# Two-layer hybrid backbone step: weighing with V as the stationary operand in two column groups, a bank for each head's transposes, and loads and splits at the layer boundary in another order

## The chip, the cores and the metric

The kernel runs on one core of one Trainium2 chip. The metric is the device time of one execution, in microseconds; several executions are timed and the median is given. One further execution is recorded by the hardware profiler.

## What is computed

640 tokens (512 latent, 128 of context) go through two layers. A layer is three parallel token mixers behind one projection (an attention with windows and sinks, a gated MLP over chunks, an attention over all keys), gated and merged, and then an expert-choice channel mixer with 16 experts. The part that the change touches is the attention:

```python
def softmax_with_sink(s, sink):                 # sink is None in the second attention
    sk = sink[:, :, None, None]
    m = jnp.maximum(jnp.max(s, axis=-1, keepdims=True), sk)
    e = jnp.exp(s - m)
    return e / (jnp.sum(e, axis=-1, keepdims=True) + jnp.exp(sk - m))

sc = jnp.einsum('bqkgd,btkd->bkgqt', qi, k) * (HEAD_DIM ** -0.5)
p = softmax_with_sink(sc, sink)
o = jnp.einsum('bkgqt,btkd->bqkgd', p, v)       # "weighing"
merged = (gates[:, :, 0] * (oa @ w_a_o) + gates[:, :, 1] * (ob @ w_b_o)
          + gates[:, :, 2] * (oc @ w_c_o))
```

Each attention has 6 query heads of 64 and 2 key heads (kv), so a kv head serves 3 query heads. All data are 32-bit floats.

## The kernel before

**Tiles and pairs.** Tokens stand in NT = 5 tiles of 128 rows (four latent, one of context). A *pair* j is one tile t, one branch br (0: windowed, 1: all keys) and one g of 0 to 2, that is the two heads (kv 0, g) and (kv 1, g). There are NP = 30 pairs in a layer. Its keys come in blocks of 128: in branch 0 three or four for the latent tiles (the cache is one of them), in branch 1 five; one for the context tile. That is 108 blocks in a layer.

**The attention loop** runs over steps j = 0 to 30, and the order on every engine is written out by hand. In step j TensorE computes scores(j) (banks 0 to 3), then turn(2j-2) and turn(2j-1), the transposes of the two heads' exponentials of pair j-1 into PSUM from column 1536 on, for both heads the same place, and then weigh(j-1), which multiplies them with V into bank 5. Between these stand three gaps, which the list FILL fills with other work: gate groups (24 matmuls into bank 6), output projections ("proj", bank 7), the gated MLP and transposes ("side" work, all through bank 7, in a fixed order with one user at a time). VectorE does in step j: peak(j), the maximum over the scores; in gap 0 its part of the filling; turned(j-1), the copy of head 0's transposes; weights(j-1), the reciprocal of the sum; and weighed(j-1), which scales bank 5 by that reciprocal while copying it into the buffer AO. ScalarE does exps(j, 0), turned(j-1) for head 1 and exps(j, 1). When the three pairs of a tile are done, the item "out" transposes AO (three transposes through bank 7) and ScalarE copies it into qoT, where the projection reads it.

Semaphores tie this together: e_ready counts exponentials, pt_done transposes, pt_evac their copies, pv_done weighings, o_evac their copies.

**The tail.** What is left of gates and projections follows the loop in a list TAIL, then the output matrix, the router, the choice of tokens and the experts.

**The experts** stream 2 MB chunks of weights through a ring of three slots on SP's queue. Every chunk is split into a rounded part (ScalarE, hi) and a rest (VectorE, lo) before TensorE uses it. POOL's queue gathers the tokens for each expert and scatters the results into x in HBM (indirect DMAs).

**The layer boundary.** ScalarE waits for the last scatter, loads x back (five tiles), squares each (L1115), takes roots (L1119), then splits two units of the projection's weights (L1141). VectorE computes means, normalises two tiles (L1471), does its part of the first split (L1459) and only then modcol (L1482, L1484), for which the evacuation of the first transposes (L1182) waits. POOL issues nine parameter loads at the start of each layer. SP loads the first two projection chunks and a chunk of the modulation weights once the last weight split of the experts is done.

**Lines.** Scores L834, transposes of exponentials L854, weighing L870, gate groups L753, projections L891, side transposes L693, modulation matmuls in four column groups of 32 L707, peak L1581 to L1586, exponentials L1248, evacuations L1259 (ScalarE) and L1594 (VectorE), weighed L1613, outputs' copy L1283, experts L1050.

Of the kernel before, what the change touches and what calls it, by code (L numbers as in the profile page):

```python
# [5 lines left out]
D = 1024  # L6
KB = D // 128
NS = 4
NT = NS + 1
DEPTH = 2  # L10
HD = 64
# [7 lines left out]
E = 16  # L19
# [122 lines left out]
for n in range(2 * NT - 1):  # L142
    put(3 * n + 4, 0, "out", n)
# [7 lines left out]
TAIL.insert(0, ("out", 2 * NT - 1))  # L151
# [6 lines left out]
def build(nc, A, outs, scratch):  # L158
# [10 lines left out]
    with ctx:  # L169
# [95 lines left out]
        AO = SC[:, 768:1536].rearrange("p (b k n) -> p b k n", b=2, k=2)  # L265
# [26 lines left out]
        psf = ps.rearrange("p b n -> p (b n)")  # L292
        s_pair = psf[:, 0:1792].rearrange("p (k c) -> p k c", k=2)
# [7 lines left out]
        PARS = 9  # L301
# [63 lines left out]
        pt_evac = sem("pt_evac")  # L365
# [156 lines left out]
        def _(pool):  # L522
# [12 lines left out]
            for l in range(DEPTH):  # L535
# [3 lines left out]
                par(wsraw, A["b_ws"][l].rearrange("g p q -> p g q"))  # L539
                par(gain.rearrange("p a b d -> p (a b d)"), A["qk_gain"][bass.ds(l, 1)].to_broadcast([128, 4 * HD]))  # L540
                par(vgain[:, :], A["b_v_norm"][bass.ds(l, 1)].to_broadcast([128, 256]))
                par(sink[:, :], A["a_sink"][bass.ds(l, 1)].to_broadcast([128, 6]))
                par(brt[:, :], A["b_router"][bass.ds(l, 1)].to_broadcast([128, E]))
                par(bs[:, :], A["b_bs"][l])
                par(cacheV[:, :, :], A["cache_v"][l])
                par(ckraw, A["cache_k"][l])
                par(wr[:, :, :], A["w_router"][l].rearrange("(k p) n -> p k n", p=128))
# [126 lines left out]
                for e in range(3):  # L674
                    gather(e)
                for e in range(E):
# [6 lines left out]
        def _(pe):  # L683
# [12 lines left out]
            for l in range(DEPTH):  # L696
# [91 lines left out]
                for g in range(QG):  # L788
# [7 lines left out]
                    if g == NT:  # L796
                        pe.wait_ge(par_ready, l * 16 * PARS + 16 * PARS)
                        side("ws", 0)
# [48 lines left out]
                def turn(v):  # L847

                    n = len(pair(v // 2)[3])
                    pe.wait_ge(e_ready, l * UNITS + v + 1)  # L850
                    if l or v:
                        pe.wait_ge(pt_evac, l * UNITS + v)
                    for i in range(n):
                        last = nc.tensor.transpose(psf[:, 1536 + 128 * i:1536 + 128 * i + 128],  # L854
# [3 lines left out]
                def weigh(j):  # L858

                    t, br, g, blocks = pair(j)  # L860
                    pe.wait_ge(pt_evac, l * UNITS + 2 * j + 2)
# [19 lines left out]
                def project(o):  # L881
# [27 lines left out]
                def outputs(n):  # L909

                    pe.wait_ge(o_evac, l * NP + 3 * n + 3)
                    side("out", n)
                    a = AO[:, n % 2].rearrange("p k n -> p (k n)")
                    transposes(7, [a[:, 128 * i:128 * i + 128] for i in range(3)], side_done)

                def merged_tile(t):

                    pe.wait_ge(merged_ready, l * 8 * NT + 7 * NT + t + 1)
                    if t == 0:
                        pe.wait_ge(e_ready, (l + 1) * UNITS)  # L920
                        pe.wait_ge(pt_evac, (l + 1) * UNITS)
                    turn_tile(H_M, t, cols2(merged[:, t]))

                def extra(kind, i):
# [9 lines left out]
                    elif kind == "out":  # L934
                        outputs(i)
# [167 lines left out]
        def _(act):  # L1103
# [7 lines left out]
            for l in range(DEPTH):  # L1111
# [13 lines left out]
                for t in range(NT):  # L1125
                    act.wait_ge(x_in[t], l * 16 + 16)
                    square(0, t)
                for t in range(NT):
                    root(t, rs5[:, t:t + 1], st5[:, t:t + 1])
# [44 lines left out]
                split(1)  # L1174
                act.wait_ge(modcol_ready, l + 1)
# [77 lines left out]
                def turned(j):  # L1253
# [5 lines left out]
                    nc.scalar.activation(probT[:, 1, 0:n], psf[:, 1536:1536 + n], ACT.Copy).then_inc(pt_evac, 1)  # L1259
# [19 lines left out]
                def outputs_out(n):  # L1279

                    br, t = divmod(n, NT)
                    act.wait_ge(side_done, l * NSIDE + SIDE["out", n] + 1)
                    nc.scalar.activation(qoT[:, 3 * br:3 * br + 3, 128 * t:128 * t + 128],  # L1283
                                         ps[:, 7, 0:384].rearrange("p (s n) -> p s n", s=3), ACT.Copy).then_inc(side_free, 1)

# [6 lines left out]
                def extra(kind, i):  # L1292
# [3 lines left out]
                    elif kind == "out":  # L1296
                        outputs_out(i)
# [107 lines left out]
        def _(dve):  # L1405
# [14 lines left out]
            for l in range(DEPTH):  # L1420
# [52 lines left out]
                for t in range(NT):  # L1473
                    mean(0, t)
                normalise(0)
                normalise(1)
                split(0)
# [8 lines left out]
                dve.wait_ge(modcol_ready, l + 1)  # L1486

# [377 lines left out]
```

## Time and profile before

| what | value |
|---|---|
| median of 3 runs | 2658.25 us (2649.14 to 2659.18) |
| the profiled execution | 2648.39 us |
| its span | 2646.6 us |
| TensorE (PE) busy | 2370.5 us, 90% |
| VectorE (DVE) busy | 1577.5 us, 60% |
| ScalarE (ACT) busy | 1195.9 us, 45% |
| DMA | 566.08 MB, 214 GB/s over the span |

Layer 0's mixers run from the start to about 740 us, its experts to 1335 us, layer 1's mixers from 1344 to about 2060 us and its experts to the end. The attention loops lie from about 211 to 548 us and from 1519 to 1858 us. Where this text counts a matmul in f32 on the trace, it is two rows, and so are its weight loads. Durations of matmuls overlap; what one takes from the engine is seen in the distance between starts.

### The profile page before, as it was taken

The numbers are of one execution on the slowest core, as the hardware profiler recorded it, in microseconds if no ns is written. First come the engines' busy times: TensorE is split into PE (matmuls) and PEld (weight loads), VectorE is DVE, ScalarE is ACT, GpSimd is POOL, SyncE is SP. The second block draws the span as 40 slices with busy tenths as digits, with TensorE's granted clock in tenths as the row PEclk, the third lists the DMA queues.
The fourth block names the chain that finished last, engine by engine and source line by source line (L and its number), as shares of the span: only waits on it lengthen the run. The fifth ranks groups of instructions, "written<-read, shape, count | busy, mean of one in ns | idle before, by whom it ended". The sixth has DMA issues, their size and how long they took to land.

```text
span 2646.6 us, 36927 instructions
## 1 busy us (share of the span) xinstructions
PE 2370.5 (90%) x14645; PEld 1837.7 (69%) x14645; DVE 1577.5 (60%) x1807; ACT 1195.9 (45%) x1368; POOL 326.4 (12%) x246
## 2 busy tenths in 40 slices
PE   3998899999859999999849988999995999999997
PEld 1777779989636666666537777898995566666664
DVE  1244434334648888888832453343246788888885
ACT  3223223222246666676632332233122666676674
POOL 1012000000020112221111020000003012111211
PEclk8999999999979999999969999999996999999998
DMA  8351110023589999999844510101044899999995
GB/s 320 128 178 49 50 57 33 4 85 136 193 294 341 369 372 367 371 376 373 320 159 160 175 52 19 56 33 57 33 175 147 288 357 370 372 380 373 370 377 187
DMA packets 268317, 566.08 MB, mean 214 GB/s; under 512 B 7496, under 2 KB 9608, under 8 KB 268144
## 3 DMA queue, kind: packets, MB, share of 16 engines
q1 hardware_dynamic: 251776, 509.63, 53.3%
q0 software_dynamic: 14512, 48.05, 6.3%
q10 hardware_dynamic: 1904, 6.62, 0.7%
q8 instruction: 92, 1.51, 0.2%
q14 instruction: 33, 0.27, 0.0%
HBM read 542.71 MB, written 24.18 MB: 214 GB/s over the span
## 4 chain that ended last, share of the span: by engine, by line
PE 35%; DMA 19%; DVE 7%; ACT 5%; issue 5%; DVEq 0%; ACTq 0%; SPq 0%; POOL 0%; POOLq 0%
PE ps L1050 13%; PE ps L753 12%; DMA ring<-in_w_down 9%; DMA ring<-in_w_up 8%; DVE w_lo L1768 5%; ACT w_hi L1360 3%; PE ps L891 3%; PE ps L870 2%; PE ps L834 1%; PE ps L693 1%; DVE EP L1783 1%; PE ps L854 1%; DMA X<-x_save 0%; PE ps L707 0%; DMA ring<-in_w_gate 0%
## 5 line engine op out<-in xcount | busy, mean ns | idle before, releaser
L1768 DVE TENSOR_TENSOR w_lo<-ring,w_hi 128x2048 fp32r<-128x2048 f32 x378 | 859.2, 2285 | 161.2 <-ACT w_hi L1360 158.4
L1360 ACT ACTIVATE w_hi<-ring 128x2048 fp32r<-128x2048 f32 x384 | 720.5, 1911 | 356.4 <-DMA ring<-in_w_down 165.1
L1050 PE MATMUL ps<-w_hi,xT 128*80 128x512 f32 x2048 | 649.9, 396 | 5.5 <-issue 3.2
L753 PE MATMUL ps<-WH,HTH 128*128 128x256 f32 x1840 | 543.8, 296 | 14.5 <-ACT Y L1277 9.0
L753 PE MATMUL ps<-ringL,HTH 128*128 128x256 f32 x1840 | 523.2, 284 | 0.0
L753 PE MATMUL ps<-WH,HTL 128*128 128x256 f32 x1840 | 522.2, 284 | 0.0
L1050 PEld LDWEIGHTS ps<-w_hi,xT 128*80 128x80 f32 x2048 | 305.9, 149 | 179.0 <-issue 9.8
L1050 PE MATMUL ps<-w_lo,xT 128*80 128x512 f32 x1024 | 405.9, 396 | 0.0
L753 PEld LDWEIGHTS ps<-WH,HTH 128*128 128x128 f32 x1840 | 355.1, 193 | 41.4 <-issue 23.4
L753 PEld LDWEIGHTS ps<-ringL,HTH 128*128 128x128 f32 x1840 | 355.4, 193 | 0.9
L753 PEld LDWEIGHTS ps<-WH,HTL 128*128 128x128 f32 x1840 | 354.2, 192 | 0.0
L1050 PE MATMUL ps<-w_hi,hT 128*80 128x512 f32 x1024 | 329.0, 397 | 25.6 <-DVE hT L1774 12.3
L1050 PEld LDWEIGHTS ps<-w_hi,hT 128*80 128x80 f32 x1024 | 153.1, 149 | 116.3 <-issue 14.7
L1050 PEld LDWEIGHTS ps<-w_lo,xT 128*80 128x80 f32 x1024 | 153.1, 150 | 80.3 <-issue 2.5
L1050 PE MATMUL ps<-w_lo,hT 128*80 128x512 f32 x512 | 203.0, 396 | 0.0
L891 PE MATMUL ps<-ring,QK 128*128 128x256 f32 x640 | 163.2, 388 | 16.0 <-ACT QK L1283 6.4
L1459 DVE TENSOR_TENSOR ringL<-ring,WH 128x2048 fp32r<-128x2048 f32 x46 | 105.4, 2290 | 111.1 <-ACT WH L1141 110.8
L891 PEld LDWEIGHTS ps<-ring,QK 128*128 128x128 f32 x640 | 112.5, 190 | 37.0 <-DVE Y L1632 9.9
L1277 ACT ACTIVATE SC<-ps 128x256 f32<-128x256 f32 x80 | 30.6, 383 | 226.9 <-PE ps L753 226.8
L1634 DVE SCALAR_TENSOR_TENSOR SC<-SC,ps 128x256 f32<-128x256 f32 x80 | 33.7, 421 | 157.9 <-PE ps L891 157.9
L1141 ACT ACTIVATE WH<-ring 128x2048 fp32r<-128x2048 f32 x46 | 87.6, 1909 | 74.0 <-PE ps L753 69.3
L671 POOL DMA_INDIRECT out<-EP,idx x16 | 62.4, 3898 | 455.0 <-DVE EP L1783 455.0
(198 smaller groups left out, 2303.7 us busy)
## 6 DMA issues: line engine op xcount, KB each, us to landing
ring<-in_w_gate SPq DMA_DIRECT2D x64, 2048.0 KB, 9.5
ring<-in_w_up SPq DMA_DIRECT2D x64, 2048.0 KB, 9.5
ring<-in_w_down SPq DMA_DIRECT2D x64, 2048.0 KB, 11.5
ring<-in_w_mod SPq DMA_DIRECT2D x23, 2048.0 KB, 7.9
ring<-in_w_in SPq DMA_DIRECT2D x18, 2048.0 KB, 7.8
ring<-in_w_out SPq DMA_DIRECT2D x4, 2048.0 KB, 9.4
ring<-in_w_o SPq DMA_DIRECT2D x4, 1536.0 KB, 6.4
Y<-x_save POOLq DMA_DIRECT2D x10, 512.0 KB, 7.1
```

The source lines that it names most:

```text
L671: pool.indirect_dma_start(x_out[l], bass.IndirectOffsetOnAxis(ap=idx[0:CE, e:e + 1], axis=0), eo[0:CE, e % 2], None, compute_op=ALU.add).t ...
L693: last = nc.tensor.transpose(ps[:, bank, 128 * i:128 * i + 128], s, ident[:, :])
L753: last = nc.tensor.matmul(dst, a[:, t, k], w, start=k == 0 and i == 0, stop=k == KB - 1 and i == 2)
L870: last = nc.tensor.matmul(ps[:, 5, 64 * kv:64 * kv + 64], probT[:, kv, 128 * i:128 * i + 128], v, start=i == 0, stop=i == len(blocks) - 1)
L891: last = nc.tensor.matmul(ps[:, 7, 0:256], qoT[:, k, 128 * t:128 * t + 128], w[:, i, 256 * q:256 * q + 256], start=i == 0, stop=k == ks[-1])
L1050: last = nc.tensor.matmul(ps[0:CE, bank], lhs[:, a, kb], w[:, u, k], start=kb == 0 and i == 0, stop=kb == KB - 1 and i == 2)
L1141: nc.scalar.activation(WH[:, u % 2], unit_cols(l, u, ring), ACT.Copy).then_inc(wa_hi, 1)
L1277: nc.scalar.activation(dst, ps[:, 6, 0:256], ACT.Tanh, scale=0.5).then_inc(gs_ready, 1)
L1360: nc.scalar.activation(w_hi[:, u % UB], ring[:, raw[0], 4 * (u % 2):4 * (u % 2) + 4], ACT.Copy).then_inc(hi_ready, 1)
L1459: TT(unit_cols(l, u, ringL), unit_cols(l, u, ring), WH[:, u % 2].bitcast(f32), ALU.subtract).then_inc(wa_lo, 1)
L1634: STT(gated, gate_s[:, o % 2], 1.0, ps[:, 7, 0:256], ALU.add, ALU.mult).then_inc(side_free, 1)
L1768: TT(w_lo[:, u % UB], ring[:, raw[0], 4 * (u % 2):4 * (u % 2) + 4], w_hi[:, u % UB].bitcast(f32), ALU.subtract).then_inc(lo_ready, 1)
```

## The change

Weighing takes V (128 keys by 64) as the stationary operand and streams the transposed weights (128 columns). The two heads of a pair go to two column groups, rows 0 to 63 and 64 to 127 of bank 5, so that the output comes out already transposed, and is copied straight into qoT. The transposes "out", their copies and AO are gone; the rows of the output weights are put in the order of the pairs on the host. As the scale of a query now lies along columns, the exponentials are scaled before they are transposed: weights(j-1) comes to the start of VectorE's step and does two multiplications. In branch 0 the two heads' transposes get a bank each. At the boundary, seven of nine parameter loads for layer 1 are issued during layer 0's experts, ScalarE's and VectorE's first splits stand ahead of the norms, the first chunks' loads wait for different counts, and the modulation chunk waits for x.

```diff
-for n in range(2 * NT - 1):
-    put(3 * n + 4, 0, "out", n)
-TAIL.insert(0, ("out", 2 * NT - 1))
-        AO = SC[:, 768:1536].rearrange("p (b k n) -> p b k n", b=2, k=2)
+        turned_at = lambda v: 1536 + (512 * (v % 2) if pair(v // 2)[1] == 0 else 0)
-        PARS = 9
+        PARS = 7
...
                 for c, slot in PRE[l]:
-                    if BEFORE[l][c] is None:
-                        sp.wait_ge(lo_ready, l * UNITS_E + 1)
-                    else:
+                    if BEFORE[l][c] is not None:
                         released(BEFORE[l][c])
+                    elif l:
+                        sp.wait_ge(lo_ready, l * UNITS_E + 1 - 2 * (RING - 1 - slot))
+                    if c == ("mod", 0):
+                        sp.wait_ge(x_in[NT - 1], 16 * (l + 1))
...
+                def load_params(l):
+                    par(gain.rearrange("p a b d -> p (a b d)"), A["qk_gain"][bass.ds(l, 1)].to_broadcast([128, 4 * HD]))
+                    par(vgain[:, :], A["b_v_norm"][bass.ds(l, 1)].to_broadcast([128, 256]))
+                    par(sink[:, :], A["a_sink"][bass.ds(l, 1)].to_broadcast([128, 6]))
+                    par(brt[:, :], A["b_router"][bass.ds(l, 1)].to_broadcast([128, E]))
+                    par(bs[:, :], A["b_bs"][l])
+                    par(cacheV[:, :, :], A["cache_v"][l])
+                    par(wr[:, :, :], A["w_router"][l].rearrange("(k p) n -> p k n", p=128))
+                raw(wsraw, A["b_ws"][l].rearrange("g p q -> p g q"))
+                raw(ckraw, A["cache_k"][l])
+                if l == 0:
+                    load_params(0)
...
                 for e in range(3):
                     gather(e)
+                if l + 1 < DEPTH:
+                    load_params(l + 1)
...
                 def turn(v):
-                    pe.wait_ge(e_ready, l * UNITS + v + 1)
-                    if l or v:
-                        pe.wait_ge(pt_evac, l * UNITS + v)
+                    pe.wait_ge(p_ready, l * UNITS + v + 1)
+                    if v // 2 >= NP // 2 or v // 2 == 0:
+                        for b in range(2):
+                            if l * NP + (v + 1 - b) // 2:
+                                pe.wait_ge(pt_evac[b], l * NP + (v + 1 - b) // 2)
+                    else:
+                        pe.wait_ge(pt_evac[v % 2], l * NP + v // 2)
...
                 def weigh(j):
-                    for kv in range(2):
-                        for i, b in enumerate(blocks):
+                    for i, b in enumerate(blocks):
+                        for kv in range(2):
...
-                            last = nc.tensor.matmul(ps[:, 5, 64 * kv:64 * kv + 64], probT[:, kv, 128 * i:128 * i + 128], v,
-                                                    start=i == 0, stop=i == len(blocks) - 1)
+                            last = nc.tensor.matmul(ps[64 * kv:64 * kv + 64, 5, 0:128], v,
+                                                    probT[:, kv, 128 * i:128 * i + 128], start=i == 0,
+                                                    stop=i == len(blocks) - 1, tile_position=(0, 64 * kv))
...
                 def project(o):
+                    if s:
+                        pe.wait_ge(o_evac, l * NP + 3 * ((s - 1) * NT + t) + 3)
...
                 # ScalarE
+                if l == 0:
+                    norms()
...
                 split(0)
                 split(1)
+                if l:
+                    norms()
...
                 # VectorE
+                if l == 0:
+                    norms()
+                    split(0)
...
                 dve.wait_ge(modcol_ready, l + 1)
+                if l:
+                    split(0)
+                    norms()
...
                 def weights(j):
+                    for kv in range(2):
+                        TS(prob[:, kv, 0:n], prob[:, kv, 0:n], rden[:, b, kv:kv + 1], None, ALU.mult).then_inc(p_ready, 1)
                 def weighed(j):
-                    TT(AO[:, n % 2, :, 64 * g:64 * g + 64], ps[:, 5, 0:128].rearrange("p (k d) -> p k d", k=2),
-                       rden[:, j % 2, :, None].to_broadcast([128, 2, HD]), ALU.mult).then_inc(o_evac, 1)
+                    nc.vector.tensor_copy(qoT[:, 3 * br + g, 128 * t:128 * t + 128], ps[:, 5, 0:128]).then_inc(o_evac, 1)
                 for j in range(NP + 1):
+                    if j:
+                        weights(j - 1)
                     if j < NP:
                         peak(j)
...
-                    if j:
-                        weights(j - 1)
```

## Rows read from the trace of the kernel before

**Rows 1.** Windows of three stages: length, busy (records) of each engine, clock, DMA

```profile
210.00:330.00 120.00, 103.05 (x776) 92.86 (x775) 55.31 (x121) 38.36 (x90) 16.24 (x25) 0.91 0.14 46
400.00:535.00 135.00, 132.35 (x1117) 125.15 (x1116) 54.27 (x101) 41.57 (x88) 0.00 (x0) 1.00 0.09 32
780.00:1000.00 220.00, 213.50 (x980) 138.06 (x981) 186.53 (x122) 149.94 (x111) 26.75 (x11) 0.99 1.02 360
```

**Rows 2.** Grouped lines of TensorE by shape: busy us, mean ns, idle before

```profile
L891 PE MATMUL ps<-ring,QK 128*128 128x256 f32 x640 | 163.2, 388 | 16.0 <-ACT QK L1283 6.4 <-DVE Y L1632 5.4 <-DVE Y L1621 3.2
L870 PE MATMUL ps<-Y,EP 128*128 128x64 f32 x672 | 92.8, 276 | 5.3 <-ACT EP L1259 5.3
L834 PE MATMUL ps<-QK 64*128 64x128 f32 x864 | 76.5, 301 | 4.8 <-ACT EP L1248 3.2 <-issue 1.6
L854 PE MATMUL ps<-ident,EP 128*128 128x128 f32 x432 | 67.4, 274 | 9.0 <-DVE EP L1594 7.7 <-ACT EP L1248 1.3
L870 PE MATMUL ps<-cacheV,EP 128*128 128x64 f32 x192 | 38.1, 281 | 0.0
...
L693 PE MATMUL ps<-ident,SC 128*128 128x128 f32 x90 | 15.5, 281 | 5.7 <-DVE Y L1632 3.1 <-ACT QK L1203 1.7 <-DVE SC L1613 0.9
```

**Rows 3.** Timeline of TensorE in the second branch, layer 0: start, duration, instruction

```profile
469.21 0.71 PE L854 MATMUL ps<-ident,EP 128*128 128x128 f32 x5
...
469.76 1.46 PE L891 MATMUL ps<-ring,QK 128*128 128x256 f32 x6
...
471.05 1.00 PE L870 MATMUL ps<-Y,EP 128*128 128x64 f32 x8
...
473.32 1.39 PE L834 MATMUL ps<-QK 64*128 64x128 f32 x20
...
474.64 0.38 PE L753 MATMUL ps<-WH,HTH 128*128 128x256 f32 x1
...
477.57 0.60 PE L854 MATMUL ps<-ident,EP 128*128 128x128 f32 x4
```

**Rows 4.** Timeline of TensorE around a modulation matmul in column groups

```profile
1391.90 0.28 PE L753 MATMUL ps<-WH,HTL 128*128 128x256 f32 x1
1392.11 1.92 PE L707 MATMUL ps<-ring,condT 128*32 128x512 f32 x16
1393.96 0.39 PE L753 MATMUL ps<-WH,HTH 128*128 128x256 f32 x1
1394.18 0.28 PE L753 MATMUL ps<-ringL,HTH 128*128 128x256 f32 x1
```

**Rows 5.** What the exponentials (L1248) waited for: us, times

```profile
PE ps L854: 62.2, 32
DVE nm L1586: 11.7, 4
```

**Rows 6.** Timeline at the layer boundary

```profile
1344.33 2.40 ACTq L1124 DMA_DIRECT2D X<-x_save  x5
...
1359.46 1.06 ACT L1115 ACTIVATE QK<-X 128x1024 f32<-128x1024 f32 x1 [1.10 <-DMA X<-x_save]
1360.42 0.19 ACT L1115 ACTIVATION_READ_ACCUMULATOR QK<-X 128x1 f32 x1
...
1362.40 3.70 ACT L1141 ACTIVATE WH<-ring 128x2048 fp32r<-128x2048 f32 x2
...
1363.21 1.94 PE L693 MATMUL ps<-ident,QK 128*128 128x128 f32 x8 [27.84 <-issue]
...
1364.33 2.29 DVE L1459 TENSOR_TENSOR ringL<-ring,WH 128x2048 fp32r<-128x2048 f32 x1 [0.36 <-ACT WH L1141]
...
1367.16 1.50 ACT L1182 ACTIVATE EP<-ps,modcol 128x128 f32<-128x128 f32 x4 [1.07 <-DVE modcol L1484]
...
1368.63 0.75 DVE L1471 TENSOR_SCALAR QK<-X,rs 128x1024 f32<-128x1024 f32 x1
```

**Rows 7.** DMA issues, 1320 to 1365 us: KB each, median us to landing

```profile
X<-x_save ACTq DMA_DIRECT2D x5, 512.0 KB, 10.1
```

More of the change, by code:

```diff
@@ L364, in build @@
         pt_done = sem("pt_done")
-        pt_evac = sem("pt_evac")
+        pt_evac = [sem(f"pt_evac{b}") for b in range(2)]
+        p_ready = sem("p_ready")
+        raw_ready = sem("raw_ready")
         pv_done = sem("pv_done")
@@ L537, in par, with raw @@
                     pool.dma_start(dst, src).then_inc(par_ready, 16)
[L539 to L547, printed above, removed]
+                def raw(dst, src):
+                    pool.dma_start(dst, src).then_inc(raw_ready, 16)
+                def load_params(l):
[10 more added lines that the diff above has]
+                    load_params(0)
                 def load_bias(i):
@@ L849, in turn @@
                     n = len(pair(v // 2)[3])
-                    pe.wait_ge(e_ready, l * UNITS + v + 1)
-                    if l or v:
-                        pe.wait_ge(pt_evac, l * UNITS + v)
+                    pe.wait_ge(p_ready, l * UNITS + v + 1)
[5 more added lines that the diff above has]
+                        pe.wait_ge(pt_evac[v % 2], l * NP + v // 2)
+                    at = turned_at(v)
                     for i in range(n):
-                        last = nc.tensor.transpose(psf[:, 1536 + 128 * i:1536 + 128 * i + 128],
+                        last = nc.tensor.transpose(psf[:, at + 128 * i:at + 128 * i + 128],
                                                    prob[:, v % 2, 128 * i:128 * i + 128], ident[:, :])
@@ L860, in weigh @@
                     t, br, g, blocks = pair(j)
-                    pe.wait_ge(pt_evac, l * UNITS + 2 * j + 2)
+                    for b in range(2):
+                        pe.wait_ge(pt_evac[b], l * NP + j + 1)
                     if l or j:
@@ L907, in mixed @@
                     transposes(7, [y[:, t, BU + 128 * i:BU + 128 * i + 128] for i in range(2)], side_done)
[L909 to L914, printed above, removed]
                 def merged_tile(t):
@@ L920, in merged_tile @@
                         pe.wait_ge(e_ready, (l + 1) * UNITS)
-                        pe.wait_ge(pt_evac, (l + 1) * UNITS)
+                        for b in range(2):
+                            pe.wait_ge(pt_evac[b], (l + 1) * NP)
                     turn_tile(H_M, t, cols2(merged[:, t]))
@@ L933, in extra @@
                         mixed(i)
-                    elif kind == "out":
-                        outputs(i)
                     else:
@@ L1124, in _, with norms @@
                         act.dma_start(x[:, t], xs_d[128 * t:128 * t + 128]).then_inc(x_in[t], 16)
[L1125 to L1129, printed above, removed]
+                def norms():
+                    for t in range(NT):
+                        act.wait_ge(x_in[t], l * 16 + 16)
+                        square(0, t)
+                    for t in range(NT):
+                        root(t, rs5[:, t:t + 1], st5[:, t:t + 1])
+                if l == 0:
+                    norms()
                 def split(u):
@@ L1471, in normalise, with norms @@
                     TS(xn[:, t % 2], x[:, t], rs5[:, t:t + 1], None, ALU.mult).then_inc(xn_ready, 1)
[L1473 to L1477, printed above, removed]
+                def norms():
+                    for t in range(NT):
+                        mean(0, t)
+                    normalise(0)
+                    normalise(1)
+                if l == 0:
+                    norms()
+                    split(0)
                 dve.wait_ge(mcol1_in, 16)
@@ L1593, in turned @@
                         dve.wait_ge(pv_done, l * NP + j)
-                    nc.vector.tensor_copy(probT[:, 0, 0:n], psf[:, 1536:1536 + n]).then_inc(pt_evac, 1)
+                    nc.vector.tensor_copy(probT[:, 0, 0:n], psf[:, 1536:1536 + n]).then_inc(pt_evac[0], 1)
                 def weights(j):
-                    br, b = pair(j)[1], j % 2
+                    t, br, g, blocks = pair(j)
+                    n, b = 128 * len(blocks), j % 2
                     dve.wait_ge(e_ready, l * UNITS + 2 * j + 2)
@@ L1605, in weights @@
                         link(nc.vector.reciprocal(rden[:, b], sm[:, b]))
+                    for kv in range(2):
+                        TS(prob[:, kv, 0:n], prob[:, kv, 0:n], rden[:, b, kv:kv + 1], None, ALU.mult).then_inc(p_ready, 1)
                 def weighed(j):
-                    n, g = divmod(j, 3)
+                    t, br, g, _ = pair(j)
                     dve.wait_ge(pv_done, l * NP + j + 1)
-                    if g == 0 and n >= 2:
-                        dve.wait_ge(side_done, l * NSIDE + SIDE["out", n - 2] + 1)
-                    TT(AO[:, n % 2, :, 64 * g:64 * g + 64], ps[:, 5, 0:128].rearrange("p (k d) -> p k d", k=2),
-                       rden[:, j % 2, :, None].to_broadcast([128, 2, HD]), ALU.mult).then_inc(o_evac, 1)
+                    nc.vector.tensor_copy(qoT[:, 3 * br + g, 128 * t:128 * t + 128], ps[:, 5, 0:128]).then_inc(o_evac, 1)
                 def mlp(t):
```

14 lines of the change are left out of this document (5 added, 9 removed).

## The prediction

> **What bounds the kernel now.** I read the run's own time first and then the windows by stage. The expert stage keeps TensorE busy for 213.5 of 220 us at a DMA share of 1.02 [rows 1]: two limits at once, and only a few loads of this change touch it. The attention stage is bound by TensorE alone: 132.35 of 135 us busy in the second attention branch, at full clock, DMA share 0.09. In the first branch it is 103.05 of 120 us, at a granted clock of 0.91, so there waits and clock take a part. VectorE is busy 54.27 of 135 us [rows 1]. So an instruction taken off TensorE in this stage is worth its spacing, and work put on VectorE is free as long as nothing comes to wait for it.
>
> The grouped lines by shape say how many instructions there are and what they waited for [rows 2]. Duration is no cost here: matmuls overlap, so I take the spacing of starts from the timeline [rows 3, 4]. The waits before the exponentials tell which side of the softmax loop is slack [rows 5], and the timeline and the landing times at the layer boundary tell what stands between the experts and the next layer [rows 6, 7].
>
> **1. Weighing.** Each block of 128 keys costs two heads, and each matmul in f32 is two instructions: 672 + 192 = 864 rows over two layers, that is 216 blocks by 4 [rows 2]. One pair of five blocks starts at 471.05, and the scores behind it at 473.32: 2.27 us for 20, or 0.1135 us each. The new form streams 128 columns where the old streamed 64, but into 64 columns of the array, two groups side by side. No such shape is in the trace. From below: four column groups of 32 with 512 columns take 1393.96 - 1392.11 = 1.85 us for 16 [rows 4], 0.116 each, so by columns and groups (512/4 against 128/2) a bound of 0.058. From above: no overlap, at the transposes' spacing, which also stream 128 columns (469.21 to 469.76 for five, 0.11). The nearest row is the scores: same 128 columns, two halves of the array, two instructions a matmul, 1.32 us for 20, or 0.066 [rows 3]. I take 0.066: 864 x (0.1135 - 0.066) = 41 us.
>
> Against it stands a change of array shape. Going into the column groups, the matmul at 1391.90 is followed at 1392.11, 0.09 later than the usual 0.12; coming back, the second matmul stands 0.22 behind the first instead of 0.12 [rows 4]. The scores already pay such a change on both sides, so a pair gets one more, at 0.1: 60 pairs, 6 us. Left: **35 us** (3 us lost without overlap; 42 at 0.058). The Trainium skill (TensorEngine Tiling (Array Packing), Key Properties) says that a change of tiling mode drains TensorE. The trace agrees that there is a price and puts it at 0.1 us; were a drain the whole rest of a matmul behind its start (0.276 long, 0.1135 spaced), it would be 0.16, and 10 us in place of 6.
>
> **2. Transposes of the outputs.** Gone are 3 for each of 10 tiles and 2 layers, 60 of the 90 rows out of that buffer, at 0.11: 6.6 us. With them go waits: 6.4 us of projections for the copy behind these transposes, and at most the 5.7 us before the transposes themselves [rows 2]. The projection will often wait for the item before instead; I take half of 12.1: together **12.6 us** (6.6 to 18.7). ScalarE's 20 copies go too, which are hidden.
>
> **3. A bank for each head.** TensorE waits 7.7 us for VectorE's evacuation between the two heads' transposes [rows 2]. Only the first branch gets two banks. I take half, **4 us** (0 to 7.7).
>
> **4. Scaling moved before the transposes.** VectorE gets two multiplications a pair, 128 to 640 columns each. Nearest row: 1024 columns in 0.75 us [rows 6]. By columns, 216 x 2 head-blocks x 128 = 55296 columns give 40 us over both layers; at 0.75 each, whatever the width, 90 us. With 60 reciprocals ahead of the next maximum, 0.2 each, that is about 0.9 us a pair. What hides it: the multiplications run while TensorE computes the next scores (1.32 us) and a gate group, and the head's transposes come only behind those. Queued behind the multiplications on VectorE is the next pair's maximum, for which the exponentials wait. Those waited 62.2 us for transposes, 32 times, and 11.7 us for the maximum, four times [rows 5]; so the maximum has room. Uncovered, it would cost 0.9 x 60 = 54 us. What comes late next: the first head's evacuation, behind a split or a projection on VectorE, and the next scores, now that weighing covers less of the second exponential. I allow **-5 us** (0 to -15) for such waits.
>
> **5. The boundary.** Four edits: two splits ahead of the norms on ScalarE, one on VectorE; seven of nine parameter loads moved into the experts of layer 0; the first projection chunk's load no longer waits for the last weight split; the modulation chunk behind the x loads. Before, the five x loads are issued from 1344.33 and the last square starts at 1359.46, then roots, transposes at 1363.21, two splits of 3.70 us on ScalarE, one of 2.29 us on VectorE, and only at 1367.16 the evacuation [rows 6]. After: ScalarE is free at 1346.7, splits to 1350.4, squares five tiles at about 1.25 (1.06 for the square, 0.19 for its read-out) to 1356.7, against 1360.6 now. The tiles should be there: 2.6 MB at the experts' 360 GB/s [rows 1] are 7.3 us, against a landing time of 10.1 each beside the parameters [rows 7]. That is 3.9 us. Then the evacuation of the first transposes (four of eight, so 1.0 of their 1.94 us, and 0.1 for the signal) follows them without splits between: 1.1 us behind instead of the 3.95 from 1363.21 to 1367.16, another 2.8. **7 us** (3 if x lands no sooner, 9 if the last scatter, now beside a chunk, also gains). Hidden: the modulation chunk, issued near 1354 instead of 1325, is first used at 1392.11 less 8; the other two loads keep their place. The wait for x on SP's queue has only chunk loads behind it, and they wait for their slots anyway.
>
> The seven loads go on POOL's queue between the third and fourth gathers. POOL has nothing there until the first expert's scatter. But the DMA engines are full [rows 1]. By the shapes of their tiles they bring 0.46 MB, 1.3 us at 360 GB/s; with small packets at most 4. **-2 us** (0 to -4). In layer 0 the order at the start hardly moves.
>
> **Sum.** 35 + 12.6 + 4 - 5 + 7 - 2 = 51.6 us. The profiled execution took 2648.4 us, so 2597 on its terms. The median of the runs, 2658.25, is 10 above it, their lowest 1 above; a median of the changed kernel would lie some 3 above its good runs: **2600 us**.
>
> **The rivals.**
> - *No overlap of the column groups* (0.12). Both groups write the same bank, and each matmul streams twice the columns. Part 1 becomes -3, the sum 14: 2638 us. Against it: four groups into one bank at 0.116 for 512 columns each [rows 4].
> - *The gain turns into waits* (0.12). TensorE's queue gets shorter per pair, the loop scores, maximum, exponential, transposes does not. For it: the first branch idles 17 of 120 us already [rows 1]. If half of parts 1 to 3 is lost: 2648.4 - 26 + 3 = 2625 us.
> - *The clock falls more often* (0.08). It stood at 0.91 over the first branch [rows 1], 11 us of 120 at most. The same again in both layers: 2600 + 22 = 2622 us; falls that vanish give 2578.
> - *Slower: VectorE sets the pace* (0.04). The multiplications stand ahead of the maximum. If the exponentials of most pairs wait for the maximum, the 0.9 us come on top in every pair and parts 1 to 3 are off the path: 2648.4 + 54 - 7 + 2 = 2697 us. It decides from where that wait is in over half of the pairs; now it is four of 120 exponentials, and a pair of the second branch has on TensorE, besides weighing and scores, at least one gate group, 2.9 us from 474.64 to 477.57 [rows 3], to cover 0.9.
>
> **Numbers.** The forecast has 0.64, its own range 2584 to 2615. The range reaches to the half-lost gain above and to the vanished clock falls below: 2578 to 2627, leaving out lack of overlap and slower. A measurement of this kernel can tell about 0.5%, 13 us. Faster holds all but VectorE's pace and part of the first rival: 0.92; same 0.04; slower 0.04.
>
> **What would show it.** In the changed profile: weighing rows 64 columns wide still 864, and a five-block pair from first weighing matmul to next scores in 1.3 to 1.4 us instead of 2.27 (rival one: 2.2). No transposes out of the old buffer but 30. Exponentials waiting for the maximum in few places. Transposes behind the x tiles of layer 1 about 4 us sooner after the x loads' issue, the evacuation 1 us behind. The expert stages unchanged within 3 us. The prediction is wrong if TensorE's idle time in the attention stages grows by more than 15 us in all, if the spacing of weighing is near 0.11, or if the clock stands under 0.9 there.

## The result and the profile after

The changed kernel takes 2576.08 us (median of 4 runs, 2570.43 to 2581.15), beside 2653.69 us for the kernel before in the same session. The ratio is 0.9713, 95% interval 0.9694 to 0.9732: 76 us, or 2.9%, faster. The forecast was 2600 us with a range down to 2578, so the sign was right and the gain too small: the sum said 51.6 us, the two profiled executions differ by 2648.39 - 2574.88 = 73.5 us.

The starts of the first and last instructions of each kind, read from TensorE's timeline, cut both executions into the same stretches:

```
us                        before   changed   difference
start to first scores      211.0     210.7      -0.3
attention, layer 0         336.3     302.2     -34.1
to first expert matmul     207.2     203.6      -3.6
experts, layer 0           580.5     577.9      -2.6
last expert matmul to
  first group of layer 1    44.9      35.8      -9.1
to first scores            139.0     139.9      +0.9
attention, layer 1         337.5     309.4     -28.1
to first expert matmul     198.5     194.5      -4.0
experts, layer 1           577.4     582.8      +5.4
last expert matmul to end   14.2      16.3      +2.1
```

The attention loops give 62 us, the boundary 9. The experts of layer 1 are the same work in both; over the profiles of this study an expert stretch took 577 to 587 us, so their +5.4 is no effect that this profile can show. The +2.1 at the end is one, and comes up again under the boundary.

First the windows of the changed kernel: branch 0 of layer 0, branch 1 of layer 0, branch 0 of layer 1 (columns as in [rows 1]).

```profile
210.70:316.00 105.30, 90.90 (x754) 79.99 (x756) 61.27 (x135) 36.56 (x88) 16.22 (x25) 0.95 0.15 52
...
367.80:513.00 145.20, 140.97 (x1288) 128.00 (x1288) 79.25 (x158) 49.04 (x103) 0.00 (x0) 1.00 0.17 59
...
1470.00:1590.50 120.50, 105.50 (x822) 92.58 (x822) 64.68 (x144) 40.03 (x97) 16.23 (x25) 0.89 0.13 46
```

Branch 1 is nearly as full as before, 97% of TensorE's time after 98%, and shorter; VectorE rose from 40% to 55% of it. The clock went up over layer 0's first branch (0.91 to 0.95) and stands at 0.89 over layer 1's.

The grouped lines of TensorE that answer to [rows 2]:

```profile
L912 PE MATMUL ps<-ring,QK 128*128 128x256 f32 x640 | 164.3, 390 | 12.1 <-DVE Y L1652 6.8 <-DVE Y L1641 3.2 <-DVE SC L1654 1.1
L846 PE MATMUL ps<-QK 64*128 64x128 f32 x864 | 76.0, 300 | 4.8 <-ACT EP L1268 3.2 <-issue 1.6
L871 PE MATMUL ps<-ident,EP 128*128 128x128 f32 x432 | 66.5, 273 | 3.8 <-issue 2.0 <-DVE EP L1628 0.8 <-DVE EP L1614 0.7
L888 PE MATMUL ps<-EP,Y 128*64 128x128 f32 x672 | 52.0, 289 | 5.8 <-issue 4.9 <-ACT EP L1280 0.8
...
L704 PE MATMUL ps<-ident,SC 128*128 128x128 f32 x30 | 4.9, 272 | 0.0
L888 PE MATMUL ps<-EP,cacheV 128*64 128x128 f32 x192 | 19.5, 282 | 0.0
```

Weighing has the same 864 rows, now 64 columns wide; of the side transposes 30 are left, with no wait before them. The projections' waits fell from 16.0 to 12.1 us, those of the exponentials' transposes from 9.0 to 3.8, and only 0.8 us in all is put down to the new scaling (L1628).

The timeline of TensorE in branch 1, against [rows 3]:

```profile
403.57 0.71 PE L871 MATMUL ps<-ident,EP 128*128 128x128 f32 x5
404.12 1.46 PE L912 MATMUL ps<-ring,QK 128*128 128x256 f32 x6
405.51 1.09 PE L888 MATMUL ps<-EP,Y 128*64 128x128 f32 x16
406.43 0.39 PE L888 MATMUL ps<-EP,cacheV 128*64 128x128 f32 x4
406.75 1.39 PE L846 MATMUL ps<-QK 64*128 64x128 f32 x20
```

From the first weighing matmul to the scores it is 1.24 us for 20, 0.062 each, where it was 2.27 us. The projection's six take 0.215 each before they are followed by another full-array matmul (469.76 to 471.05 in [rows 3], 1.29 us); here it is 1.39 to the first weighing matmul: the further change of array shape costs 0.1.

### The profile page after: what moved, and what is told of

Its sections match the earlier page's. It is cut to its first block, busy times and chain, and to the rows that moved or that the text cites. A ratio compares the mean times of both kernels' runs of the same rounds, so it can differ in the third digit from the quotient of the medians.

```text
span 2573.1 us, 36937 instructions
## 1 busy us (share of the span) xinstructions
PE 2313.4 (90%) x14585; PEld 1768.8 (69%) x14585; DVE 1634.4 (64%) x1927; ACT 1187.8 (46%) x1348; POOL 336.7 (13%) x246
## 4 chain that ended last, share of the span: by engine, by line
PE 57%; DMA 20%; DVE 10%; issue 7%; ACT 6%; DVEq 0%; SPq 0%; ACTq 0%; POOL 0%; POOLq 0%
PE ps L764 25%; PE ps L1063 14%; DMA ring<-in_w_up 8%; DMA ring<-in_w_down 7%; PE ps L912 6%; DVE w_lo L1788 5%; ACT w_hi L1372 3%; PE ps L846 3%; PE ps L888 2%; DMA ring<-in_w_gate 2%; PE ps L871 1%; PE ps L704 1%; PE ps L718 1%; DMA ring<-in_w_mod 1%; PE ps L982 1%
## 5 line engine op out<-in xcount | busy, mean ns | idle before, releaser
L764 PE MATMUL ps<-WH,HTH 128*128 128x256 f32 x1840 | 541.1, 294 | 14.8 <-ACT Y L1298 9.1
L912 PE MATMUL ps<-ring,QK 128*128 128x256 f32 x640 | 164.3, 390 | 12.1 <-DVE Y L1652 6.8
L680 POOL DMA_INDIRECT x_save<-EP,idx x16 | 65.0, 4060 | 454.5 <-DVE EP L1803 454.5
```

Source lines behind the costliest of these rows:

```text
L680: pool.indirect_dma_start(x_out[l], bass.IndirectOffsetOnAxis(ap=idx[0:CE, e:e + 1], axis=0), eo[0:CE, e % 2], None, compute_op=ALU.add).t ...
L764: last = nc.tensor.matmul(dst, a[:, t, k], w, start=k == 0 and i == 0, stop=k == KB - 1 and i == 2)
L912: last = nc.tensor.matmul(ps[:, 7, 0:256], qoT[:, k, 128 * t:128 * t + 128], w[:, i, 256 * q:256 * q + 256], start=i == 0, stop=k == ks[-1])
```

## The experiments

The step lengths below are distances between the starts of neighbouring scores on TensorE's timeline. Wherever the clock is full they repeat to some 0.02 us from kernel to kernel, step 0 excepted, which differs by 0.8 us between kernels without a pattern and is not counted below. Steps up to 14 belong to branch 0; from step 16 on, the pairs weighed are of branch 1, in the steps shown mostly with five blocks.

```
us, layer 0, step             2      3      4     16     17     18     22     24     25
before                     10.60  11.39  11.92  11.40  11.75  10.21  11.32  10.21  13.08
changed                     9.19   9.97   9.88   9.27  10.81   9.27   9.59   9.27  10.97
one group after the other   9.45  10.25  10.35   9.97  11.51   9.98   9.98   9.98  11.66
outputs' item back          9.18   9.98  11.06  10.47  10.80   9.28  11.11   9.27  12.09
the same, short copy        9.18   9.98  10.75  10.15  10.80   9.27  10.79   9.27  11.78
one place for transposes   10.08  10.86   9.88   9.27  10.80   9.28   9.59   9.27  10.96
maximum first               9.19   9.97   9.88  10.45  10.81  10.44  10.83  10.44  12.01
scaled twice                9.19   9.98   9.88   9.27  10.81   9.34  10.76   9.34  12.14
```

### The boundary alone

The kernel before with all edits at the boundary and none in the attention: parameter loads, SP's waits, and the splits ahead of the norms (diffs under the two halves below).

> The kernel before with the four boundary edits alone. Theory: in the changed profile the stretch from the experts' last matmul to layer 1's first group is 9.2 us shorter than before (35.75 against 44.9), and nothing else of these edits shows, so this kernel is 9 us faster than before (8 to 11). Rival: the surplus over the forecast came from the boundary edits in some other place (the experts of layer 0, the chunks' loads), then 15 us or more. Second rival: the boundary's 9 us are partly the attention's doing, then 3 to 5 us.

Measured: ratio 0.9976 (0.9959 to 0.9994), 6 us; the boundary stretch went from 44.9 to 35.8 us, and layer 0's experts, with the seven loads in them, took 580.6 us beside 580.5. So the boundary is worth 9 us where it stands, and the surplus over the forecast is not there.

Of these 9 us the end of the program takes 2 back. The last instruction of POOL's queue, behind the last scatter, takes 6808 ns in the kernel before and 8727 ns in the changed one:

```profile
L169 POOLq DRAIN  x1: 6808/6808/6808, 2639.5 to 2639.5; - x1
L166 POOLq DRAIN  x1: 8727/8727/8727, 2564.1 to 2564.1; - x1
```

The profiles fall into two sets: 6808 ns in the kernel before, with the attention alone and with the splits only, 8727 ns wherever the loads were changed, this kernel among them. So the 1.9 us belong to the edits of the loads; which of them does it was not tried. 9.1 less 1.9 is 7.2 us, and the runs say 6.

### The attention alone

The changed kernel with the boundary as it was.

> The changed kernel with the boundary as before: only the attention's part of the change. Theory: two attention loops and two tails lose 66 us in the changed profile (weighing 39, the outputs' item 23, the bank for each head 4), so this kernel is 64 us faster than before, ratio 0.976 (0.973 to 0.979). Rival (my forecast's terms 1 to 4, 46.6 us): ratio 0.982.

Measured: 0.9729 (0.9707 to 0.9751), 72 us. The terms 1 to 4 of the forecast, 46.6 us, would be 0.982 and are outside the interval. The miss is in the attention. Its loops took 302.2 and 303.7 us; every step outside the clock's falls has the length that it has in the changed kernel.

### One column group after the other

```diff
-                    for i, b in enumerate(blocks):
-                        for kv in range(2):
+                    for kv in range(2):
+                        for i, b in enumerate(blocks):
```

> The changed kernel, with weighing's two loops exchanged: all blocks of the first head, then all of the second, so that neighbouring matmuls stand in the same column group. Theory (the gain is the overlap of the two groups): the five-block pair takes from 1.24 us to 2.2 us from its first weighing matmul to the next scores, and the kernel is slower than the changed one by 216 x 4 x 0.048 = 41 us, ratio to before about 0.987. Rival (narrower weights or the longer stream alone give the spacing of 0.062): pair stays at 1.3 us, ratio 0.971.

Measured: 0.9785 (0.9762 to 0.9807), 19 us slower than the changed kernel, half of what I expected; the steps add up to 25. The timeline of this kernel's weighing:

```profile
390.21 1.15 PE L888 MATMUL ps<-EP,Y 128*64 128x128 f32 x10
391.14 0.27 PE L888 MATMUL ps<-EP,cacheV 128*64 128x128 f32 x1
391.19 0.27 PE L888 MATMUL ps<-EP,Y 128*64 128x128 f32 x1
391.25 0.27 PE L888 MATMUL ps<-EP,cacheV 128*64 128x128 f32 x1
391.30 0.71 PE L888 MATMUL ps<-EP,Y 128*64 128x128 f32 x5
391.85 0.38 PE L888 MATMUL ps<-EP,cacheV 128*64 128x128 f32 x2
392.16 1.39 PE L846 MATMUL ps<-QK 64*128 64x128 f32 x20
```

20 rows take 1.95 us, not 2.2, and still the two groups overlap here, at the seam. A head has eight rows with Y and then two with cacheV. Ten rows with Y start before the first with cacheV at 391.14, so two of them are already head 1's. Read row by row, head 0 starts from 390.21 to 391.25 and head 1 from 390.93 to 391.96; within a head the starts stand 0.109 us apart behind the first, like the transposes, which stream as many columns. In the changed kernel the rows come in twos, 0.007 apart and 0.102 to the next two: each group again has 0.109 a row, and the other group's rows come for nothing.

If head 1 had waited for its turn, it would have started at 391.36 and not at 390.93, 0.43 us later, and the pair would have taken about 2.3 to 2.4 us (an estimate), no less than the 2.27 of the kernel before. So the gain of 0.94 us in a step with a five-block pair (step 18) is the overlap: 0.71 need the alternating order (9.98 against 9.27), and the 0.23 that are left without it come from the seam. The 41 us expected left the seam out.

### The outputs' item put back

```diff
+for n in range(2 * NT - 1):
+    put(3 * n + 4, 0, "out", n)
+TAIL.insert(0, ("out", 2 * NT - 1))
...
+                def outputs(n):
+                    br, t = divmod(n, NT)
+                    pe.wait_ge(o_evac, l * NP + 3 * n + 3)
+                    side("out", n)
+                    transposes(7, [qoT[:, 3 * br + i, 128 * t:128 * t + 128] for i in range(3)], side_done)
...
+                    nc.scalar.activation(AO[:, 0:384], ps[:, 7, 0:384], ACT.Copy).then_inc(side_free, 1)
```

> The changed kernel with the outputs' item put back in its old places: three transposes through bank 7 and a copy of 384 columns on ScalarE, into a spare buffer. Theory: each of the 20 items costs 1.17 us of TensorE's queue (0.33 for the transposes, 0.67 for the wait of the projection behind them, the rest signals), 23 us in all, ratio to before 0.980. Rival (the forecast, half of the waits come back anyway): 12.6 us, ratio 0.976.

Measured: 0.9785 (0.9762 to 0.9809), 19 us slower than the changed kernel. Steps 4, 10, 13 and 16 grow by 1.18 to 1.20 us each, 19 by 0.27, 22 by 1.52, 25 by 1.12, 28 by 1.29. With step 7, where the clock's fall moved (7 and 8 together +0.37), the nine items inside a loop cost near 9.3 us, and the tenth, after the loop, 1.7 (from the last weighing to the next projection it is 2.04 us in this kernel, 0.37 in the changed one): 22 us over two layers. The forecast had 12.6. Who waited for the item's copy, in this kernel:

```profile
PE ps L916: 6.8, 12
PEld ps L916: 2.4, 4
PEld ps L708: 0.8, 2
PE ps L925: 0.5, 2
```

These waits, with 6.6 us of transposes, come to 17 us. The other 5 the views do not book; the item's own start behind the copy of the item before, the signals, and other work moved late would be candidates, and none was measured.

### The outputs' item with a copy of one column

The kernel above, with `AO[:, 0:1]` and `ps[:, 7, 0:1]` in the copy.

> The changed kernel with the outputs' item put back, but ScalarE copies one column instead of 384 (0.49 us by the trace of before, here about 0.2). Theory: what the item costs TensorE is its transposes plus the way of bank 7 through ScalarE and back, so a step with the item is 0.3 us shorter than with the full copy (10.47 us for step 16) and 0.9 longer than without (9.27). Rival: the copy's length does not matter, the item costs its place in the order of bank 7: step 16 stays at 10.4 to 10.5 us.

Measured: 0.9745 (0.9728 to 0.9761). The copy fell from 491 to 171 ns, and step 16 to 10.15 us: 0.32 less than with the full copy, 0.88 more than without the item. So of the item's 1.20 us 0.32 go with the copy's length and 0.33 are three transposes; the 0.55 that are left would be the way of bank 7 through ScalarE and back to the projection, which no run takes apart. Here steps and times part: the steps with the tenth items add up to 17 us over the changed kernel, the times to 8. Three others go the same way: 19 timed and 25 by steps (one group after the other), 19 and 22 (item put back), 15 and 20 (maximum first, below). The changed kernel's own profile has 5.7 us of longer falls of the clock in layer 1, which the others have not (see the clock below), and the experts' stretches differ by some us from profile to profile; which of them it is was not tried. The sums below go by the steps.

### One place for both heads' transposes in branch 0

```diff
-        turned_at = lambda v: 1536 + (512 * (v % 2) if pair(v // 2)[1] == 0 else 0)
+        turned_at = lambda v: 1536
...
-                    if v // 2 >= NP // 2 or v // 2 == 0:
+                    if True:
```

> The changed kernel, with the two heads' transposes of branch 0 in one place again and the waits that go with it. Theory: the second head's transposes wait about 0.74 us for VectorE's copy again in those steps of branch 0 that have nothing in gap 1 (three a layer), so steps 2 and 3 of each layer take 9.9 and 10.7 us instead of 9.18 and 9.98, and all in all 4 to 5 us are lost, ratio to before about 0.973. Rival: VectorE, which now scales before, is late with that copy in many steps, and the bank for each head is worth 10 us or more.

Measured: 0.9713 (0.9695 to 0.9731), no difference from the changed kernel that the times could tell. The steps show it: 2 and 3 grow by 0.89 us each, those behind them not at all, 1.8 us a layer and 3.6 in all. The first theory stands, with two places a layer instead of three, each a little dearer.

### The maximum before the scaling

```diff
-                    if j:
-                        weights(j - 1)
                     if j < NP:
                         peak(j)
+                    if j:
+                        weights(j - 1)
```

> The changed kernel, but VectorE takes the next pair's maximum first and scales the exponentials behind it. Theory: scaling is off the path in either place, since gate groups and projections lie between scores and transposes; the steps keep their lengths within 0.1 us, ratio to before 0.970 to 0.973. Rival (scaling ahead of the maximum delays the exponentials): steps get shorter by some tenths, 5 to 15 us in all. Second rival: now the transposes wait for the scaling in steps whose gap 0 holds only a projection (1.3 us), and the kernel is 5 to 20 us slower than the changed one.

Measured: 0.9771 (0.9757 to 0.9786), 15 us slower than the changed kernel: the second rival. Its waits before the exponentials' transposes:

```profile
L871 PE MATMUL ps<-ident,EP 128*128 128x128 f32 x432 | 67.2, 275 | 21.5 <-DVE EP L1628 17.2 <-issue 3.6 <-DVE EP L1614 0.7
```

and the place, in step 16 (VectorE's maximum, the two multiplications, and TensorE's transposes after a wait of 0.96 us):

```profile
381.46 1.56 PE L912 MATMUL ps<-ring,QK 128*128 128x256 f32 x6
381.57 1.49 DVE L1601 TENSOR_REDUCE mx<-ps 128x2 f32<-128x1280 f32 x1 [1.02 <-PE ps L846]
383.10 0.17 DVE L1606 TENSOR_SCALAR nm<-mx 128x2 f32<-128x2 f32 x1
383.18 0.16 DVE L1626 RECIPROCAL rden<-sm 128x2 f32<-128x2 f32 x1
383.37 1.02 DVE L1628 TENSOR_SCALAR EP<-EP,rden 128x640 f32<-128x640 f32 x2
383.98 0.76 PE L871 MATMUL ps<-ident,EP 128*128 128x128 f32 x5 [0.96 <-DVE EP L1628]
```

Steps 15, 16, 18, 20, 22, 24, 25 and 26 grow by 1.0 to 1.2 us; in the even ones gap 0 holds only a projection. Steps 17, 19, 21 and 23, with a gate group there, keep their length. (Step 10 grows by 0.6.) The order of the two on VectorE is worth 15 to 20 us, and my first theory, that either order is covered, fell.

### Scaled twice

```diff
+                        link(TS(SC[:, 768:768 + n], prob[:, kv, 0:n], rden[:, b, kv:kv + 1], None, ALU.mult))
                         TS(prob[:, kv, 0:n], prob[:, kv, 0:n], rden[:, b, kv:kv + 1], None, ALU.mult).then_inc(p_ready, 1)
```

> The changed kernel; VectorE scales every head twice, the first time into a spare buffer, so 0.5 us more before each head's transposes and 1.1 us more before each maximum of a five-block pair, some 45 us of VectorE's time in all. Theory: VectorE has room for the scaling in the changed kernel; of 45 us doubled under 10 come out, since the maximum's delay is covered by gate groups but not where gap 0 holds only a projection. Rival (my forecast's fourth rival, VectorE close to setting the pace): 25 us or more, with the exponentials waiting for the maximum in over half of the pairs.

Measured: 0.9738 (0.9718 to 0.9758), some 7 us slower than the changed kernel; the steps add up to 6.5 us (22 and 25 grow by 1.17 each, behind or beside one of VectorE's splits, 15 by 0.3, most others by 0.07 or nothing). What the exponentials waited for, first in the changed kernel and then in this one (us, times):

```profile
PE ps L871: 57.7, 35
DVE nm L1606: 22.3, 6
```

```profile
DVE nm L1606: 83.1, 20
PE ps L871: 10.4, 21
```

The exponentials now wait 83.1 us for the maximum, and most of TensorE's steps do not change: the exponentials are done before TensorE has worked off what stands between. The cost is the first theory's; by count the maximum is late in 20 of the 60 pairs, not in half.

### The boundary's halves

Splits only:

```diff
                 # ScalarE and VectorE, layer 1
+                if l == 0:
+                    norms()
                 split(0)
                 split(1)
+                if l:
+                    norms()
```

> The kernel before, with only the order at layer 1's start changed: ScalarE's two splits and VectorE's split stand ahead of the norms; all loads as before. Theory (the forecast's own second half of part 5): the x loads land as late as before, the last square ends as before, and only the splits between transposes and evacuation go: the boundary shrinks from 44.9 to about 42.1 us, 2.8 us. Rival (the splits also fill the time in which ScalarE waits for x, which is worth nothing more, but their 3.7 us push the squares behind the last landing): 1.5 us or less.

Loads only:

```diff
-                        sp.wait_ge(lo_ready, l * UNITS_E + 1)
+                        sp.wait_ge(lo_ready, l * UNITS_E + 1 - 2 * (RING - 1 - slot))
+                    if c == ("mod", 0):
+                        sp.wait_ge(x_in[NT - 1], 16 * (l + 1))
...
+                if l + 1 < DEPTH:
+                    load_params(l + 1)
```

> The kernel before, with only the loads changed: seven parameter loads in layer 0's experts, the ring's chunks by their new waits. Theory: last scatter and x loads find empty queues; the last scatter lands 2.3 us sooner, the last square 4 us or more sooner than that (ScalarE is not held up by splits here, so it follows the landings), the boundary shrinks from 44.9 to 37 to 39 us, and layer 0's experts keep their 580 us within 3. Rival (the x loads' time is their own, not the others' traffic): the boundary stays above 42 us.

Measured: 0.9997 (0.9985 to 1.001) and 0.9979 (0.9960 to 0.9997). The stretch is 41.7 us with the splits only, 3.2 less, and 37.5 us with the loads only, 7.4 less; together 9.1. That they do not add up is seen on ScalarE of the changed kernel, where two splits and five squares follow one another with no wait for x in between (start of layer 1, against [rows 6]):

```profile
1303.90 3.71 ACT L1159 ACTIVATE WH<-ring 128x2048 fp32r<-128x2048 f32 x2 [23.81 <-issue]
1307.52 1.04 ACT L1128 ACTIVATE QK<-X 128x1024 f32<-128x1024 f32 x1
...
1312.47 1.06 ACT L1128 ACTIVATE QK<-X 128x1024 f32<-128x1024 f32 x1
...
1316.23 1.94 PE L704 MATMUL ps<-ident,QK 128*128 128x128 f32 x8 [21.43 <-issue]
...
1317.41 1.51 ACT L1202 ACTIVATE EP<-ps,modcol 128x128 f32<-128x128 f32 x4 [1.90 <-PE ps L704]
```

In the kernel with the loads alone the runs say 5.6 us: 7.4 less the 1.9 at the program's end. The x loads of the changed kernel, their issue and their landing times, against [rows 6, 7]:

```profile
1301.46 2.40 ACTq L1137 DMA_DIRECT2D X<-x_save  x5
...
X<-x_save ACTq DMA_DIRECT2D x5, 512.0 KB, 7.2
```

## Why the prediction fell short

Step by step, as the prediction put it, over both layers:

| part | forecast | shown | from |
|---|---|---|---|
| 1 weighing | 35 | 36 to 38.5 | steps, and pair 2.27 to 1.24 + 0.1 |
| 2 outputs' transposes | 12.6 | 22 | item put back; timed 19 |
| 3 bank for each head | 4 | 3.6 | steps of one place |
| 4 scaling | -5 | about 0 | steps, scaled twice |
| 5 boundary | 7 | 9.1 | boundary alone |
| 5 loads in the experts | -2 | 0 | 580.5 to 580.6 us |
| not in it: the program's end | none | -1.9 | POOL's last instruction |
| not in it: falls of the clock | none | 5 to 6, -2 in the changed profile | estimate, see below |
| sum | 51.6 | 69 to 71 without the clock | profiles: 73.5; runs: 76 |

**The step that failed is part 2**, the outputs' transposes: the mechanism was right, the term was mis-sized by 10 us, 22 shown for 12.6, and lies above even the upper bound that it had, 18.7. It took the waits from one line's view of TensorE's matmuls and then halved them. The item costs a link in a serial chain: bank 7 has one user at a time, so transposes, ScalarE's copy and the next projection follow one another, 1.2 us in most places. The part booked to weight loads (3.2 us with the item put back) and the part booked to nobody (5) were not in the sum. And less came back than the half that was assumed: the projections' 6.4 us of waits for the item's copy are gone and their waits for others grew by 2.5 (16.0 to 12.1 in all), the 5.7 us before the side transposes are gone whole, so 9.6 of 12.1 went.

**Part 1** held nearly to the number: by spacing 864 x (0.1135 - 0.062) - 6 = 38.5 us; by steps 10.4 us for branch 1 in each layer (162.2 us from step 15 to the last weighing before, 151.8 with the outputs' item put back) and, at 0.73 and 0.52 us for pairs of four and three blocks (0.94 brought down by blocks), 7.5 for branch 0, 36 us. The nearest row, the scores' 0.066, was close to 0.062; the further change of array shape cost the 0.1 that the modulation matmuls had shown. The first rival, no overlap at all, did not occur; its price, the whole of part 1, is what the spacing of 0.109 within a group bears out, though no run is without overlap at the seam.

**Part 4** allowed 5 us for new waits; none came that the steps would show. What covers the scaling was named rightly (the next scores and the gap's filling), but of two orders only this one has it: the maximum first costs 15 us. The fourth rival is far off. Even with the scaling doubled the maximum is late in 20 pairs only, and its 83.1 us of waiting cost the kernel 7 us, since the exponentials have slack of their own; its turning point, half of the pairs, was not reached and stays untested.

**Part 5** was right in its two halves: from the issue of the x loads to the first transposes it was 18.9 us and is 14.8 (1301.46 to 1316.23), 4.1 for the forecast's 3.9, and from there to the evacuation 3.95 and 1.18, the forecast's 2.8; the splits alone gave 3.2. It was short by the last scatter: from the last expert matmul to the issue of the x loads it was 9.3 us before; in the kernel with the loads alone 7.0 (1335.81 to 1342.84). The forecast had that only as the end of its range. That the loads into the full queues of the experts cost nothing is shown within the 3 us by which those stretches differ at the least. What they did cost, 1.9 us at the program's end, was not in the sum.

**The clock** is the term that the sum put at nothing. Somewhere in steps 5 to 9 the granted clock falls from 2.4 to 1.2 GHz; the stretch ahead of the fall and the fall itself, in layer 0 of the kernel before and then of the changed one (columns as in [rows 1]):

```profile
275.60:285.83 10.23, 8.64 (x72) 7.45 (x71) 8.40 (x18) 3.70 (x11) 0.00 (x0) 1.00 0.02 8
285.83:296.07 10.24, 10.24 (x51) 9.22 (x50) 2.66 (x10) 0.18 (x2) 1.16 (x2) 0.50 0.04 13
...
302.20:312.41 10.21, 8.62 (x79) 7.50 (x78) 4.93 (x14) 2.19 (x6) 0.00 (x0) 1.00 0.01 2
312.41:315.82 3.41, 3.41 (x22) 2.29 (x21) 0.42 (x1) 0.61 (x3) 0.00 (x0) 0.50 0.00 0
```

In the four profiles with the old attention every loop has a fall of 10.2 us in steps 5 and 6 (the splits alone another behind it). Of the sixteen loops with the new weighing twelve have one of 3.4 us, one has two such, two have none, and only layer 1 of the changed kernel has two of 10.2 (clock 0.89; the loop is 5.7 us longer than in the kernel with the attention alone, 303.7 us). One of 3.4 us costs 1.6 us (step 8, 12.80 with the attention alone, 11.17 at full clock), one of 10.2 us 4.3 to 4.6 (steps 5 and 6, 8 and 9 of that layer 1). By these prices, an estimate, the shorter falls are worth 5 to 6 us over two layers in most of these kernels, while the changed kernel's own profile gains 3 in layer 0 and loses 4 to 5 in layer 1. So the third rival had the sign wrong for most loops, and only one loop has the clock under 0.9 that the prediction named as a sign against it. TensorE had been busy 8.6 of 10.2 us ahead of either fall; why the falls became shorter was not tried.

The other two signs did not appear: the spacing is 0.062, and TensorE's idle time in the loops fell, from 27.9 and 28.3 us to 22.5 and 22.6. So the second rival, gain turned into waits, is out.

## What to carry to other kernels

A small item in a chain that passes one buffer between engines costs the whole round trip, not its instructions: size it by the distance from the work before to the work behind, as in a step with it against a step without it. When a matmul's moving side is 64 columns and its stationary side 128, exchange them and alternate column groups; the gain is the overlap of the groups, and without the alternation over half of it is gone. An edit at one place can cost at another: compare the profiles to their very end. Where work moves onto a second engine, ask which of its two waiting customers has slack, and put the other first.

## What was not expected of the hardware

Two column groups used in turn with 128 columns each run at 0.062 us a row, while each group by itself keeps 0.109. With the groups one behind the other TensorE started rows of the second group 0.32 us before the last of the first (390.93 and 391.25), against the program's order, so that a pair of heads still took 1.95 us and not 2.3. The closing instruction of POOL's queue took 6808 or 8727 ns, to the nanosecond, by whether the loads had been changed. A copy cut from 384 columns to one, 491 to 171 ns, took 0.32 us from the chain and left 0.88: more than half of such a hand-over is not the copy. The last scatter lands about 2.3 us sooner when no chunk loads stand beside it.
